# Expert gates from rounded one-hots in a high and a low part, and delta-rule scalings spread over four jobs

## Chip, cores and metric

The program runs on one core of one Trainium2 chip. Its metric is the device time of one execution in microseconds (us), the median of the runs shown. TensorE (PE), VectorE (DVE), ScalarE (ACT) and GpSimd (POOL) run their own instruction streams in order and meet at semaphores; SyncE (SP) issues most DMAs.

## What is computed

One block with attention, a state-space mixer, memory attention and an expert layer is followed by two layers with a state-space duality mixer, latent attention, a gated delta rule and an MLP. There are 512 tokens of width 1024. Two places matter here.

The expert layer scores 128 first keys and 128 second keys for each of 8 heads, takes the best 16 pairs, and weighs 16384 experts by them:

```
sv, si = lax.top_k(s, PEER_TOPK)                      # per side, 16 of 128
top, pos = lax.top_k(cand, PEER_TOPK)                 # 16 of the 256 sums
g = jax.nn.softmax(top, axis=-1)
act = jax.nn.gelu(jnp.einsum('thkd,td->thk', u_tab[e], xb))
return jnp.einsum('thk,thkd->td', (g * act), v_tab[e])
```

The delta rule solves, per head and chunk of 128 tokens, a triangular system, and needs the values and keys of each head turned (tokens on partitions) and scaled by beta and by decays.

## The kernel before

**The expert layer (`choose_and_dot`).** For 384 of the 512 tokens all experts are computed densely. The stage multiplies the tokens with 128 weight tiles ("dots"); a tile is 8 chunks, a chunk three products of 128x128 weights with 384 tokens (high x high, low x high, high x low, all in the rounded format fp32r; lines 104 to 106). For every tile, ACT makes the high part of the weights (line 541) and DVE or POOL the low part (lines 553 and 562), PE multiplies, and ACT applies Gelu (line 1889).

Beside it a gate matrix is built. For each token there is a matrix 128x128 over (second key, first key) that holds the gate of every chosen pair. It is the product of two one-hot matrices over the 128 chosen pairs: `hotB`, which is 1 where the pair's second key is the column, and `hotA`, which is the gate where its first key is the column. Both are fp32. Tokens are taken in groups of four. For a group, DVE makes `hotA` with four instructions (is_equal, then mult; line 2031) and `hotB` with one (line 2033), PE multiplies (`gates`, line 1851, four products in fp32), and ACT copies the bank to the gate block (`fill`, line 1894). Both one-hots have two buffers (`HOTS = 2`), so DVE may be two groups ahead; the banks allow PE four groups ahead of ACT.

There are three blocks of 32 groups (blocks 1, 2, 3; block 0 has none, its tokens go another way). PE's order in a block is written out: some tiles (`EARLY_DOTS`, 13 or 14), three transposes of the chosen keys and gates (line 1861), one more tile, then 32 times a group's gates and five chunks. ACT's order for a group is `fill(g)`, and after each tile `after_dot` (a high part and a Gelu); five tiles end in eight groups. DVE's order for a group is the one-hots, one dot product of gathered rows (line 2018), and a low part when one is due. Between the gate stages DVE chooses the pairs of the next block.

**The delta rule (`delta_rule`).** Each of two layers runs it for two halves of four heads, so it runs four times. A half inverts its triangular matrices in 24 jobs (6 levels by 4 heads). A job is, in order: POOL makes a masked matrix (line 3136), PE a product `w` (line 3018), ACT a copy of it (line 3159), PE a product `v` (line 3031), DVE an update (line 3245), PE a transpose back (line 3051), and DVE two masked copies (lines 3215 and 3250). PE's loop issues `w(j+1)`, then `v(j)`, then `turn_back(j-1)`. In every fourth job (4, 8, 12, 16) PE also turns one head: 4 transposes of values and 4 of keys in one go (line 3043, between `w` and `v`). ACT scales the turned values with four instructions after its copy of one job (line 3166) and the turned keys with four after the copy of the next (line 3173); the second set waits for DVE, which first reads the turned keys for `gdn_kd` (line 3257).

Of the kernel before, what the change touches and what calls it, by code (L numbers as in the profile page):

```python
# [11 lines left out]
ALU = mybir.AluOpType  # L12
# [1697 lines left out]
def choose_and_dot(nc, dram, weights, xnH, xnL, iota, room, qT, keys, hT, scratch, banks, ident, spare, rstd, pairs, A, act_pair):  # L1710
# [7 lines left out]
    with ExitStack() as held:  # L1718
# [3 lines left out]
        hotA, hotB = sb("first_hot", [P, HOTS, TOKENS, PK]), sb("second_hot", [P, HOTS, TOKENS, PK])  # L1722
# [52 lines left out]
        with stage(nc, "spilled scored kept dve_step logits exps gates_ready turned laid hot used tokens_done block_filled "  # L1775
                       "activated block_stored x_turned x_laid rows_ready rows_used pairs_activated " + " ".join(names)) as (
                block, spilled, scored, kept, dve_step, logits, exps, gates_ready, turned, laid, hot, used, tokens_done, filled,
                activated, block_stored, x_turned, x_laid, rows_ready, rows_used, pairs_activated, *act_stored, early_loaded, early_weighed, early_high):
# [40 lines left out]
            def _(pe):  # L1819
# [26 lines left out]
                def gates(m):  # L1846
                    pe.wait_ge(hot, m + 1)
                    if m >= 4:
                        pe.wait_ge(filled, m - 3)
                    for k in range(TOKENS):  # L1850
                        last = nc.tensor.matmul(banks[2 + m % 4][:, k * P:(k + 1) * P], hotB[:, m % HOTS, k, :], hotA[:, m % HOTS, k, :],
                                                start=True, stop=True)
                    last.then_inc(tokens_done, 1)
# [17 lines left out]
            def _(act):  # L1871
# [18 lines left out]

                def fill(t, g):
# [7 lines left out]
                for t in range(TT):  # L1899
# [6 lines left out]
                    for k, dst in enumerate((first, second, gateT)):  # L1906
                        nc.scalar.copy(dst[:, t * P:(t + 1) * P], banks[6][:, k * P:(k + 1) * P]).then_inc(laid, 1)
                    after_dot(first_dot[t] + EARLY_DOTS[t])
# [3 lines left out]
                    for g in groups_of(t):  # L1912
                        fill(t, g)
                        while (done + 1) * DC <= (g + 1 - groups_of(t)[0]) * chunks_beside(t):
# [32 lines left out]
            def _(dve):  # L1947
# [22 lines left out]
                def choose(t):  # L1970
# [13 lines left out]

                    cand = s1[:].rearrange("p (h two) n -> p h (two n)", two=2)
# [35 lines left out]
                for t in range(TT):  # L2021
                    choose(t)
                    dve.wait_ge(laid, 3 * t + 3)
                    lows = [i for i in on_vector if gate_dot[t] < i - 1 < first_dot[t + 1]]
                    for g in groups_of(t):
# [4 lines left out]
                        for k in range(TOKENS):  # L2030
                            v.tensor_scalar(hotA[:, m % HOTS, k, :], iota, first[:, n + k:n + k + 1], gateT[:, n + k:n + k + 1],
# [873 lines left out]
def delta_rule(nc, dram, psum, layer, yT, vT, small, cum, row_parts, pick, smallN, cumN, col, cst, ones, ring, weights, rstd, banks, ident, scratch, tools,  # L2905
# [3 lines left out]
    with ExitStack() as held:  # L2909
# [56 lines left out]
        for hb in range(2):  # L2966
# [7 lines left out]
            with stage(nc, "rows_spread products_done masked exps ends_done dve_step banks_used ends_exp odd_turned packed halves_loaded "  # L2974
                           "pool_step firsts_by_pool first_by_dve kbs_ready level_ready w_done w_copied v_done updated t_turned t_copied "
                           "kv_turned v_scaled k_decayed k_scaled n_turned n_made m_made odd_made solved u_copied wt_copied "
# [3 lines left out]
                    turned, v_scaled, k_decayed, k_scaled, n_turned, n_made, m_made, odd_made, solved, u_copied, wt_copied,  # L2980
# [518 lines left out]
```

## Time and profile before

| what | value |
|---|---|
| median of 3 runs | 4693.05 us (4687.57 to 4697.0) |
| the profiled execution's own time | 4697.76 us |
| its span, first to last instruction | 4695.7 us |
| mean granted TensorE clock | 0.984 of full speed |
| busy share PE / DVE / ACT / POOL | 95% / 67% / 36% / 21% |
| gate stages, 868 to 1335 us | three blocks |
| jobs of the delta rule | four times some 41 us, from 2081.7, 2169.1, 3454.5 and 3542.4 us |

A busy share counts the time in which an engine has an instruction under way. Matmuls overlap in the pipeline, so a busy PE can still be paced by something else; the distances between starts tell more. One fp32 matmul is recorded as two pairs of a weight load (PEld) and a matmul, one rounded matmul as one pair.

### The profile page before, as it was taken

Reading aid. Unit: us, or ns where it says so; the run is one execution under the profiler, and the core shown is the slowest. Engines: PE = TensorE matmul, PEld = TensorE weight load, DVE = VectorE, ACT = ScalarE, POOL = GpSimd, SP = SyncE. Lnnn points to the kernel's source line nnn. Section 1 sums busy time; section 2 is a strip of 40 time slices with the busy share of each in tenths; the row PEclk is TensorE's granted clock in tenths of the full one; section 3 lists DMA queues with packets and bytes.
Section 4 is the critical chain, followed back from the end, with each engine's and each line's share of the span. In section 5 each row is a group of like instructions: output and inputs, shape, how many; then the busy total and the mean of one; then the engine's idle time right before and its main releaser. Section 6 shows DMA issues by size and latency. Waiting matters only on the chain. (4 is left out here: it accounts for less than half of the span.)

```text
span 4695.7 us, 60725 instructions
## 1 busy us (share of the span) xinstructions
PE 4484.2 (95%) x23048; PEld 3821.8 (81%) x23048; DVE 3126.7 (67%) x5382; ACT 1712.0 (36%) x2853; POOL 970.1 (21%) x934
## 2 busy tenths in 40 slices
PE   9889899999999999988999999999988999999999
PEld 7428689999999999877777778888877777878887
DVE  6576757899978888876555665533776655665443
ACT  4414433334333333433333343422423424353332
POOL 4661005664633333022000011000022010020000
PEclk9999999999999999989999999999999999999999
DMA  3002125798989999410222213233201221313332
GB/s 117 27 36 93 52 90 164 254 304 278 308 294 354 335 340 338 141 35 19 86 70 66 77 50 114 93 96 98 90 5 46 86 80 41 94 46 111 100 95 81
DMA packets 236465, 610.74 MB, mean 130 GB/s; under 512 B 23312, under 2 KB 108560, under 8 KB 235024
## 3 DMA queue, kind: packets, MB, share of 16 engines
q1 hardware_dynamic: 199312, 472.62, 31.4%
q0 software_dynamic: 36864, 134.23, 7.9%
q8 instruction: 185, 3.03, 0.3%
q14 instruction: 104, 0.85, 0.1%
HBM read 557.22 MB, written 49.55 MB: 129 GB/s over the span
## 5 line engine op out<-in xcount | busy, mean ns | idle before, releaser
L553 DVE TENSOR_TENSOR weight_low<-ring,weight_high 128x1024 fp32r<-128x1024 f32 (+2 forms) x648 | 759.9, 1173 | 940.3 <-PE banks L106 888.5
L541 ACT CAST weight_high<-ring 128x1024 fp32r<-128x1024 f32 (+2 forms) x728 | 730.0, 1004 | 541.8 <-PE banks L106 530.7
L104 PE MATMUL banks<-x_high,weight_high 128*128 128x512 f32 x1856 | 758.0, 408 | 30.1 <-DVE weight_low L553 17.0
L106 PE MATMUL banks<-x_high,weight_low 128*128 128x512 f32 x1856 | 726.5, 391 | 0.0
L105 PE MATMUL banks<-x_low,weight_high 128*128 128x512 f32 x1856 | 726.4, 391 | 0.0
L104 PEld LDWEIGHTS banks<-x_high,weight_high 128*128 128x128 f32 x1856 | 350.7, 189 | 122.5 <-issue 26.8
L553 POOL TENSOR_TENSOR weight_low<-ring,weight_high 128x1024 fp32r<-128x1024 f32 (+1 forms) x22 | 50.4, 2295 | 1927.6 <-PE banks L106 1844.9
L105 PEld LDWEIGHTS banks<-x_low,weight_high 128*128 128x128 f32 x1856 | 351.0, 189 | 82.1 <-issue 10.6
L106 PEld LDWEIGHTS banks<-x_high,weight_low 128*128 128x128 f32 x1856 | 350.4, 189 | 74.7
L104 PE MATMUL banks<-xn_high,weight_high 128*128 128x384 f32 x1024 | 353.6, 345 | 16.4 <-POOL weight_low L562 15.7
L105 PE MATMUL banks<-xn_low,weight_high 128*128 128x384 f32 x1024 | 343.1, 335 | 0.0
L106 PE MATMUL banks<-xn_high,weight_low 128*128 128x384 f32 x1024 | 343.1, 335 | 0.0
L104 PE MATMUL banks<-act_high,weight_high 128*128 128x384 f32 x688 | 233.1, 339 | 2.3 <-PEq L61 2.3
L106 PE MATMUL banks<-act_high,weight_low 128*128 128x384 f32 x688 | 232.4, 338 | 0.0
L105 PE MATMUL banks<-act_low,weight_high 128*128 128x384 f32 x688 | 232.4, 338 | 0.0
L1700 POOL DMA_INDIRECT rows_v<-in_peer_v,pair_rows x128 | 152.2, 1189 | 369.1 <-DVE pair_sum L2204 327.4
L1700 POOL DMA_INDIRECT scratch<-in_peer_u_rows,pair_rows x128 | 172.1, 1344 | 225.4 <-DVE pair_weight L2018 214.3
L104 PEld LDWEIGHTS banks<-xn_high,weight_high 128*128 128x128 f32 x1024 | 193.1, 189 | 22.4 <-POOL weight_low L562 21.5
L562 POOL TENSOR_TENSOR weight_low<-ring,weight_high 128x256 fp32r<-128x256 f32 x232 | 193.1, 865 | 59.0 <-PE banks L106 58.7
L104 PE MATMUL banks<-up_high,weight_high 128*128 128x512 f32 x512 | 199.2, 389 | 0.0
L105 PE MATMUL banks<-up_low,weight_high 128*128 128x512 f32 x512 | 199.2, 389 | 0.0
L106 PE MATMUL banks<-up_high,weight_low 128*128 128x512 f32 x512 | 199.2, 389 | 0.0
(679 smaller groups left out, 9707.3 us busy)
## 6 DMA issues: line engine op xcount, KB each, us to landing
ring<-in_peer_u SPq DMA_DIRECT2D x128, 512.0 KB, 4.6
ring<-in_peer_v SPq DMA_DIRECT2D x128, 512.0 KB, 5.5
ring<-in_w_up SPq DMA_DIRECT2D x64, 512.0 KB, 3.6
ring<-in_w_down SPq DMA_DIRECT2D x64, 512.0 KB, 3.5
ring<-in_w_gate SPq DMA_DIRECT2D x48, 512.0 KB, 3.6
acts<-dot_act SPq DMA_DIRECT2D x124, 192.0 KB, 4.0
activations<-acts SPq DMA_DIRECT2D x124, 192.0 KB, 5.6
ring<-in_w_gdn_in SPq DMA_DIRECT2D x34, 512.0 KB, 3.6
```

Of the source, the lines that this page charges most:

```text
L104: nc.tensor.matmul(out, w_high, x_high, start=start, stop=False)
L105: nc.tensor.matmul(out, w_high, x_low, start=False, stop=False)
L106: return nc.tensor.matmul(out, w_low, x_high, start=False, stop=stop)
L541: self.nc.scalar.copy(self.wH[:, g % HIGHS, 0:kc * P], self.ring[:, g % SLOTS, 0:kc * P]).then_inc(self.high_made, 1)
L553: ops.tensor_tensor(self.wL[:, g % LOWS, 0:kc * P], self.ring[:, g % SLOTS, 0:kc * P], self.wH[:, g % HIGHS, 0:kc * P].bitcast(F32), ALU.s ...
L562: last = ops.tensor_tensor(self.wL[:, g % LOWS, w], self.ring[:, g % SLOTS, w], self.wH[:, g % HIGHS, w].bitcast(F32), ALU.subtract)
L1700: self.nc.gpsimd.indirect_dma_start(out, None, table, where).then_inc(self.loaded[row_home(k, turn)], 16)
```

## The change

In the expert layer both one-hots get the rounded type, and the gate is split: `hotA` holds the gate's high (rounded) part and is made by ACT, and a new `hotL` holds the rest and is made by DVE with the same instructions as `hotA` before. ACT makes a group's `hotA` with four `Abs(iota - first)` and, after these are complete, four `Relu(gate - gate * distance)`. PE multiplies `hotB` with both and adds in the bank: eight rounded products for the four fp32 ones. Per block there are also three more small ACT instructions and one of DVE. ACT makes the first two groups right after the transposes are copied, ahead of the next tile's `after_dot`, and then group g+2 after `fill(g)`.

In the delta rule the transposes of values come in jobs 4, 8, 12, 16 and those of keys one job later. ACT's scalings come two to a job over four jobs; DVE's `gdn_kd` and `gdn_qg` come one job later.

The diff without the lines that only name semaphores:

```diff
--- before.py
+++ after.py
@@ -1719,7 +1719,10 @@
         def sb(name, shape, dt=F32):
             return held.enter_context(nc.sbuf_tensor(name, shape, dt))
         first, second, gateT = spare[:, 0, :], spare[:, 1, :], rstd
-        hotA, hotB = sb("first_hot", [P, HOTS, TOKENS, PK]), sb("second_hot", [P, HOTS, TOKENS, PK])
+        hotA, hotB = (sb(n, [P, HOTS, TOKENS, PK], F32R) for n in ("first_hot", "second_hot"))
+        hotL = nc.alloc_sbuf_tensor_at("first_hot_low", [P, HOTS, TOKENS, PK], F32R, offset=SCORES_AT)
+        gate_high = sb("gate_high", [P, P], F32R)
+        offsets, negated = first[:, 0:P], second[:, 0:P]
         s1 = nc.alloc_sbuf_tensor_at("pair_scores", [P, 2 * PH, PK], F32, offset=SCORES_AT)
         sv = sb("key_top", [P, 2 * PH, TOP])
         si = sb("key_index", [P, 2 * PH, TOP], U32)
@@ -1773,9 +1776,9 @@
...
@@ -1845,11 +1848,14 @@
 
                 def gates(m):
                     pe.wait_ge(hot, m + 1)
+                    pe.wait_ge(first_ready, m + 1)
                     if m >= 4:
                         pe.wait_ge(filled, m - 3)
                     for k in range(TOKENS):
-                        last = nc.tensor.matmul(banks[2 + m % 4][:, k * P:(k + 1) * P], hotB[:, m % HOTS, k, :], hotA[:, m % HOTS, k, :],
-                                                start=True, stop=True)
+                        nc.tensor.matmul(banks[2 + m % 4][:, k * P:(k + 1) * P], hotB[:, m % HOTS, k, :], hotA[:, m % HOTS, k, :],
+                                         start=True, stop=False)
+                        last = nc.tensor.matmul(banks[2 + m % 4][:, k * P:(k + 1) * P], hotB[:, m % HOTS, k, :], hotL[:, m % HOTS, k, :],
+                                                start=False, stop=True)
                     last.then_inc(tokens_done, 1)
 
                 for t in range(TT):
@@ -1888,6 +1894,17 @@
                         act.wait_ge(act_stored[n % 4], 16 * (n // 4))
                     nc.scalar.activation(A[:, n % 4, :], banks[n % 2][:, 0:DENSE], ACT.Gelu).then_inc(activated, 1)
 
+                def build(t, g):
+                    m, n = place[t, g], g * TOKENS
+                    for k in range(TOKENS):
+                        last = nc.scalar.activation(hotA[:, m % HOTS, k, :], iota, ACT.Abs, bias=offsets[:, n + k:n + k + 1])
+                    last.then_inc(distances, 1)
+                    act.wait_ge(distances, m + 1)
+                    for k in range(TOKENS):
+                        last = nc.scalar.activation(hotA[:, m % HOTS, k, :], hotA[:, m % HOTS, k, :].bitcast(F32), ACT.Relu, scale=negated[:, n + k:n + k + 1],
+                                                    bias=gate_high[:, n + k:n + k + 1].bitcast(F32))
+                    last.then_inc(first_ready, 1)
+
                 def fill(t, g):
                     m = place[t, g]
                     act.wait_ge(tokens_done, m + 1)
@@ -1905,12 +1922,22 @@
                     act.wait_ge(turned, t + 1)
                     for k, dst in enumerate((first, second, gateT)):
                         nc.scalar.copy(dst[:, t * P:(t + 1) * P], banks[6][:, k * P:(k + 1) * P]).then_inc(laid, 1)
+                    if groups_of(t):
+                        nc.scalar.mul(offsets, banks[6][:, 0:P], -1.0).then_inc(laid_aside, 1)
+                        nc.scalar.copy(gate_high[:], banks[6][:, 2 * P:3 * P]).then_inc(laid_aside, 1)
+                        act.wait_ge(laid_aside, 3 * blocks.index(t) + 2)
+                        nc.scalar.mul(negated, gate_high[:].bitcast(F32), -1.0).then_inc(laid_aside, 1)
+                        act.wait_ge(laid_aside, 3 * blocks.index(t) + 3)
+                        for g in groups_of(t)[:HOTS]:
+                            build(t, g)
                     after_dot(first_dot[t] + EARLY_DOTS[t])
                     if t in blocks[1:]:
                         act.wait_ge(block_stored, 16 * PARTS * blocks.index(t))
                     done = 0
                     for g in groups_of(t):
                         fill(t, g)
+                        if g + HOTS in groups_of(t):
+                            build(t, g + HOTS)
                         while (done + 1) * DC <= (g + 1 - groups_of(t)[0]) * chunks_beside(t):
                             after_dot(gate_dot[t] + done)
                             done += 1
@@ -1982,6 +2009,8 @@
                     top16(link, 2 * PH, scores[t], sv, si)
                     link(v.tensor_tensor(marked[:], si[:], marks[:].unsqueeze(1).to_broadcast([P, 2 * PH, TOP]), ALU.bitwise_or))
 
+                    if t in blocks[1:]:
+                        dve.wait_ge(tokens_done, place[t - 1, P // TOKENS - 1] + 1)
                     cand = s1[:].rearrange("p (h two) n -> p h (two n)", two=2)
                     by_side = sv[:].rearrange("p (h two) a -> p h two a", two=2)
                     link(v.tensor_tensor(cand.rearrange("p h (a b) -> p h a b", b=TOP),
@@ -2021,6 +2050,11 @@
                 for t in range(TT):
                     choose(t)
                     dve.wait_ge(laid, 3 * t + 3)
+                    if groups_of(t):
+                        block = slice(t * P, (t + 1) * P)
+                        dve.wait_ge(laid_aside, 3 * blocks.index(t) + 2)
+                        v.tensor_tensor(gateT[:, block], gateT[:, block], gate_high[:].bitcast(F32), ALU.subtract).then_inc(low_laid, 1)
+                        dve.wait_ge(low_laid, blocks.index(t) + 1)
                     lows = [i for i in on_vector if gate_dot[t] < i - 1 < first_dot[t + 1]]
                     for g in groups_of(t):
                         m = place[t, g]
@@ -2028,7 +2062,7 @@
                             dve.wait_ge(tokens_done, m - HOTS + 1)
                         n = t * P + g * TOKENS
                         for k in range(TOKENS):
-                            v.tensor_scalar(hotA[:, m % HOTS, k, :], iota, first[:, n + k:n + k + 1], gateT[:, n + k:n + k + 1],
+                            v.tensor_scalar(hotL[:, m % HOTS, k, :], iota, first[:, n + k:n + k + 1], gateT[:, n + k:n + k + 1],
                                             ALU.is_equal, ALU.mult)
                         v.tensor_tensor(hotB[:, m % HOTS], iota.unsqueeze(1).to_broadcast([P, TOKENS, PK]), bc(second[:, n:n + TOKENS], PK),
                                         ALU.is_equal).then_inc(hot, 1)
@@ -3031,17 +3065,23 @@
                             last = nc.tensor.matmul(banks[4 + j % 2][:, p * P:(p + 1) * P], second_half(x)[:, p, :], Wb[j % 2][:, p, :], start=True, stop=True)
                         last.then_inc(v_done, 1)
 
-                    def turn(x):
+                    def turn_v(x):
                         if x:
-                            pe.wait_ge(v_scaled, x)
-                            pe.wait_ge(k_scaled, x)
+                            pe.wait_ge(v_scaled, 2 * x)
                         else:
                             pe.wait_ge(t_copied, B4)
-                        for n, src in enumerate((vT[:, heads[x]], xp[:, 4 + heads[x] // 2])):
-                            for t in range(TT):
-                                s = slice(t * P, (t + 1) * P)
-                                last = nc.tensor.transpose(banks[6 + n][:, s], src[:, s], ident)
-                        last.then_inc(turned, 1)
+                        for t in range(TT):
+                            s = slice(t * P, (t + 1) * P)
+                            last = nc.tensor.transpose(banks[6][:, s], vT[:, heads[x], s], ident)
+                        last.then_inc(v_turned, 1)
+
+                    def turn_k(x):
+                        if x:
+                            pe.wait_ge(k_scaled, 2 * x)
+                        for t in range(TT):
+                            s = slice(t * P, (t + 1) * P)
+                            last = nc.tensor.transpose(banks[7][:, s], xp[:, 4 + heads[x] // 2, s], ident)
+                        last.then_inc(k_turned, 1)
 
                     def turn_back(j):
                         pe.wait_ge(updated, j + 1)
@@ -3075,8 +3115,11 @@
                             turn_first(B4 - 1)
                         if j + 1 < total:
                             w(j + 1)
-                        if j >= 4 and j % 4 == 0 and j // 4 <= B4:
-                            turn(j // 4 - 1)
+                        x, step = divmod(j - 4, 4)
+                        if 0 <= x < B4 and step == 0:
+                            turn_v(x)
+                        if 0 <= x < B4 and step == 1:
+                            turn_k(x)
                         v(j)
                         if j >= 1:
                             turn_back(j - 1)
@@ -3161,17 +3204,17 @@
                         if 0 <= x < B4:
                             h = heads[x]
                             if step == 0:
-                                act.wait_ge(turned, x + 1)
-                                for t in range(TT):
+                                act.wait_ge(v_turned, x + 1)
+                            if step == 2:
+                                act.wait_ge(k_decayed, x + 1)
+                                act.wait_ge(kbs_ready, 1)
+                            for t in (2 * (step % 2), 2 * (step % 2) + 1):
+                                if step < 2:
                                     last = nc.scalar.activation(vb[:, x, t, :], tiles4(banks[6])[:, t, :], ACT.Copy,
                                                                 scale=smallN[:, t, BETA_ROWS + h:BETA_ROWS + h + 1])
-                                last.then_inc(v_scaled, 1)
-                            if step == 1:
-                                act.wait_ge(k_decayed, x + 1)
-                                act.wait_ge(kbs_ready, 1)
-                                for t in range(TT):
+                                else:
                                     last = nc.scalar.activation(kb[:, x, t, :], tiles4(banks[7])[:, t, :], ACT.Copy, scale=kbs[:, t, x:x + 1])
-                                last.then_inc(k_scaled, 1)
+                            last.then_inc(v_scaled if step < 2 else k_scaled, 1)
 
                     for x in range(B4):
                         act.wait_ge(solved, x + 1)
@@ -3252,10 +3295,10 @@
                             v.tensor_tensor(final(x, 1), inverse(x), half_mask(LEVELS), ALU.mult).then_inc(odd_made, 1)
                         y, step = divmod(j - 5, 4)
                         if 0 <= y < B4:
-                            if step == 0:
-                                dve.wait_ge(turned, y + 1)
+                            if step == 1:
+                                dve.wait_ge(k_turned, y + 1)
                                 v.tensor_tensor(kd[:, y], tiles4(banks[7]), bc(g_end[:, y, :], P), ALU.mult).then_inc(k_decayed, 1)
-                            if step == 2:
+                            if step == 3:
                                 v.scalar_tensor_tensor(qg[:, y, :], xp[:, heads[y] // 2, 0:T], GDN_SCALE, eg[:, y].rearrange("p t n -> p (t n)"),
                                                        ALU.mult, ALU.mult)
                     turned_half(total - 1)
```

## Rows read from the trace of the kernel before

**Rows 1.** The page: busy time of each engine over the span.

```profile
PE 4484.2 (95%) x23048; PEld 3821.8 (81%) x23048; DVE 3126.7 (67%) x5382; ACT 1712.0 (36%) x2853; POOL 970.1 (21%) x934
```

**Rows 2.** Busy time by stretch: start and end, length, busy us and instructions of PE, PEld, DVE, ACT, POOL, clock.

```profile
900.00:950.00 50.00, 50.00 (x332) 50.00 (x331) 50.00 (x109) 19.95 (x31) 19.80 (x14) 1.00 0.85 282
```

**Rows 3.** Timeline, 878 to 911 us: start, length, engine, line, tiles, shape, count.

```profile
881.09 1.11 DVE L2031 TENSOR_SCALAR first_hot<-iota,spare,rstd 128x128 f32<-128x128 f32 x4
...
883.26 1.05 PE L1851 MATMUL banks<-first_hot,second_hot 128*128 128x128 f32 x8
...
884.50 0.34 PE L106 MATMUL banks<-xn_high,weight_low 128*128 128x384 f32 x1
884.68 0.33 PE L104 MATMUL banks<-xn_high,weight_high 128*128 128x384 f32 x1
...
909.00 1.11 DVE L2031 TENSOR_SCALAR first_hot<-iota,spare,rstd 128x128 f32<-128x128 f32 x4
...
911.22 0.49 PE L1851 MATMUL banks<-first_hot,second_hot 128*128 128x128 f32 x3
```

**Rows 4.** Groups of ACT instructions, 868 to 1335 us: busy us, mean ns, idle before.

```profile
L541 ACT CAST weight_high<-ring 128x1024 fp32r<-128x1024 f32 x89 | 93.6, 1052 | 0.0
L1894 ACT COPY gate_block<-banks 128x512 f32<-128x512 f32 x96 | 56.4, 587 | 178.1 <-PE banks L1851 178.1
L1889 ACT ACTIVATE dot_act<-banks 128x384 f32<-128x384 f32 x88 | 43.5, 494 | 99.9 <-PE banks L106 99.5
```

**Rows 5.** ACT instructions by form over the span, with and without an operand per partition.

```profile
L2625 ACT CAST ident_r<-ident 128x128 fp32r<-128x128 f32 x2 | 0.6, 282 | 0.0
L541 ACT CAST weight_high<-ring 128x256 fp32r<-128x256 f32 x32 | 13.0, 407 | 41.8 <-PE banks L106 40.3 <-DMA ring<-in_w_mla_uv 1.4
L609 ACT ACTIVATE mem_high<-qkT,vec 128x256 fp32r<-128x256 f32 x8 | 3.3, 496 | 1.0 <-PEq L61 1.0
```

**Rows 6.** Timeline, 2090 to 2098 us: a delta-rule job with key scalings, and one after.

```profile
2090.68 0.68 DVE L3257 TENSOR_TENSOR gdn_kd<-banks,gdn_end 128x512 f32<-128x512 f32 x1
...
2091.40 1.14 ACT L3173 ACTIVATE hT<-banks,gdn_kbs 128x128 f32<-128x128 f32 x4 [1.80 <-DVE gdn_kd L3257]
...
2092.42 0.66 ACT L3159 COPY ring<-banks 128x256 f32<-128x256 f32 x2
2092.86 0.71 PE L3031 MATMUL banks<-ring,gdn_Tt 128*128 128x128 f32 x4 [1.44 <-ACT ring L3159]
```

**Rows 7.** Timeline of DVE, 1036 to 1048 us: dependent instructions, and the wait before the one-hots.

```profile
1037.09 0.29 DVE L2005 TENSOR_REDUCE gate_sums<-to_turn 128x8 f32<-128x128 f32 x1
1037.41 0.20 DVE L2006 RECIPROCAL gate_sums<-gate_sums 128x8 f32<-128x8 f32 x1
...
1044.08 2.26 DVE L2031 TENSOR_SCALAR first_hot<-iota,spare,rstd 128x128 f32<-128x128 f32 x4 [6.13 <-ACT rstd L1907]
```

**Rows 8.** Weight loads: the timeline at 2012.65 us, and groups by form over the span.

```profile
2012.65 2.54 PEld L155 LDWEIGHTS banks<-columns,gdn_squares 128*128 128x128 f32 x21
...
L1851 PEld LDWEIGHTS banks<-first_hot,second_hot 128*128 128x128 f32 x768 | 98.6, 191 | 3.1 <-DVE second_hot L2033 3.1
...
L106 PEld LDWEIGHTS banks<-xn_high,weight_low 128*128 128x128 f32 x1024 | 192.6, 188 | 0.0
```

**Rows 9.** Table loads of ACT over the span.

```profile
L1889 ACT ACT_TABLE_LOAD x5 | 6.4, 1283 | 0.1
L1904 ACT ACT_TABLE_LOAD x4 | 5.1, 1283 | 0.1
```

**Rows 10.** Delta-rule jobs: busy by stretch, waits of the first stretch, and the copies over the span.

```profile
2081.68:2122.08 40.40, 33.65 (x255) 32.49 (x255) 30.50 (x73) 16.77 (x56) 18.22 (x21) 0.89 0.00 1
...
ACT hT L3173 <- DVE gdn_kd L3257: 8.4, 4, 2.4
...
PE banks L3031 <- ACT ring L3159: 6.7, 4, 1.9
...
  PE banks L3031: 27.0, 16
```

More of the change, by code:

```diff
@@ L1775, in choose_and_dot @@
         with stage(nc, "spilled scored kept dve_step logits exps gates_ready turned laid hot used tokens_done block_filled "
-                       "activated block_stored x_turned x_laid rows_ready rows_used pairs_activated " + " ".join(names)) as (
+                       "activated distances_made first_hot_ready laid_aside low_laid block_stored x_turned x_laid rows_ready rows_used pairs_activated " + " ".join(names)) as (
                 block, spilled, scored, kept, dve_step, logits, exps, gates_ready, turned, laid, hot, used, tokens_done, filled,
-                activated, block_stored, x_turned, x_laid, rows_ready, rows_used, pairs_activated, *act_stored, early_loaded, early_weighed, early_high):
+                activated, distances, first_ready, laid_aside, low_laid, block_stored, x_turned, x_laid, rows_ready, rows_used, pairs_activated, *act_stored, early_loaded, early_weighed, early_high):
             @block.sync
@@ L2975, in delta_rule @@
                            "pool_step firsts_by_pool first_by_dve kbs_ready level_ready w_done w_copied v_done updated t_turned t_copied "
-                           "kv_turned v_scaled k_decayed k_scaled n_turned n_made m_made odd_made solved u_copied wt_copied "
+                           "v_turned k_turned v_scaled k_decayed k_scaled n_turned n_made m_made odd_made solved u_copied wt_copied "
                            "state_ready ws_done v_new_ready o_done ds_done o_copied decayed") as (
@@ L2979, in delta_rule @@
                     pool_step, firsts_by_pool, first_by_dve, kbs_ready, level_ready, w_done, w_copied, v_done, updated, t_turned, t_copied,
-                    turned, v_scaled, k_decayed, k_scaled, n_turned, n_made, m_made, odd_made, solved, u_copied, wt_copied,
+                    v_turned, k_turned, v_scaled, k_decayed, k_scaled, n_turned, n_made, m_made, odd_made, solved, u_copied, wt_copied,
                     state_ready, ws_done, v_new, o_done, ds_done, o_copied, decayed):
```

## The prediction

> **What bounds the kernel now.** I read the busy line of the page first [rows 1]: PE 95%, DVE 67%, ACT 36%. These are means over stages, so they only say that ACT looks free. The change acts in two stages, and each has to be read for itself.
>
> The gate stages come next, by busy time per stretch [rows 2]. In a typical 50 us PE is busy 50.00, DVE 50.00 and ACT 19.95. The reader is to see that two engines are full, not one. The timeline gives their pace [rows 3]. PE starts the products of one group at 883.26 and those of the group eight later at 911.22: 27.96 / 8 = 3.495 us a group. DVE starts its one-hots at 881.09 and eight groups later at 909.00: 27.91 / 8 = 3.489 us, and in this stretch nobody makes it wait. So PE paces the stage and DVE follows 0.006 us behind. ACT needs 19.95 / (50 / 3.495) = 1.39 us a group and then waits for PE: 178.1 us in all before its fills [rows 4].
>
> In the delta rule I read the waits and the timeline of one job [rows 6, 10]. ACT holds its next copy back behind four key scalings, which themselves wait 1.80 us for DVE's gdn_kd, and PE stands 1.44 us before it can start the product that reads the copy. Over the four halves PE waits 27.0 us in 16 such places, one for each head turned.
>
> **Gates, PE's part.** A chunk is three products 0.173 us apart (884.50 to 884.68 is one step; five chunks and the gates must fill 3.495). Fifteen take 2.59 us, which leaves 3.495 - 2.59 = 0.90 us for a group's gates. They are eight pairs of load and matmul now and eight after: four fp32 products of two pairs each against eight rounded ones of one pair. What is streamed gets shorter, but what of the weight load? Where the moving side is one column, 21 loads take 2.54 us in all, so (2.54 - 0.19) / 20 = 0.117 us apart; the gate products are (1.05 - 0.28) / 7 = 0.11 apart with 128 columns [rows 3, 8]. So the load alone explains the distance today, and a load for a rounded product is recorded at 188 ns against 191 [rows 8]. I take the eight pairs at the same 0.90 us. Bounds: 8 x 0.065 = 0.52 if only the streaming counted (0.173 for 384 columns is 0.120 more than for 128 at the same rate per column, less what a product has of fixed cost), and 8 x 0.22 = 1.76 if a short rounded product streamed twice as slowly as an fp32 pair. Even the lower bound brings nothing by itself: DVE's 3.489 us stands right behind PE's 3.495, and DVE keeps its four small instructions and its large one. At most 0.006 x 96 = 0.6 us can be gained here while DVE stays.
>
> **Gates, ACT's part.** This is new and large: eight activations for each group. No row shows one from SBUF with 128 columns and two operands per partition, so I build it up. Without such an operand 128x128 takes 282 ns. One operand per partition costs 496 - 407 = 89 ns more at 256 columns [rows 5]. So an Abs (bias) takes 0.371 us and a Relu (scale and bias) 0.460. Instructions in a row overlap: four scalings of 368 ns took 1.14 us [rows 6], so they start (1.14 - 0.37) / 3 = 0.257 apart, an overlap of 0.111. Then four Abs are 3 x 0.260 + 0.371 = 1.15; the wait until they are complete adds 0.03 (a dependent instruction on DVE starts at 1037.41 after one that ended at 1037.38 [rows 7]); four Relu are 4 x 0.349 = 1.40. Together 2.58 us a group, and with the old 1.39 ACT needs 3.97 us where PE needs 3.495. ACT becomes the bound. Bounds: all eight as cheap as the PSUM scalings, 8 x 0.257 + 0.11 + 0.03 = 2.20, gives 3.59; no overlap at all, 4 x 0.371 + 0.03 + 4 x 0.460 = 3.35, gives 4.74.
>
> It will be more than the bare sum, because ACT's work comes in lumps in a fixed order. Three groups in eight have only fill and build, 0.50 + 2.58 = 3.1 us, and there ACT waits for PE. The other five carry a high part and a Gelu on top, 3.1 + 1.36 = 4.4 us. If nothing of the idle time is carried over, the mean is (5 x 4.4 + 3 x 3.5) / 8 = 4.1. A late high part then stops DVE at its low part, the next one-hots are queued behind that on DVE, which has no slack, and PE waits for them, which makes the next fill late. I put 0.1 us on this and take 4.20 us a group. The two groups of lead are used up within the first few groups. Cost: (4.20 - 3.495) x 96 = +68 us. By the bare sum of 3.97 it is +46, by the low end with lumps some +20, by the high end +120.
>
> The Trainium skill prices the same thing in "ScalarE: Activation LUTs", What ACT_TABLE_LOAD costs: about 93 ns for each pointer operand, and about 93 ns of overlap between activations in a row. The rows agree on the first (89 ns) and show a little more overlap (111 ns). By the page's figures an Abs would come every 0.293 us and a Relu every 0.386, the build would be an estimated 2.9 us, ACT 4.3, and with the same lumps the cost near +90.
>
> The small things: three extra ACT instructions a block (about 0.3 us each) and the first two builds (5.2 us) come before a tile's high part, while PE has one tile of 4.14 us and its first gates ahead of it; the third tile's high part is then made about 2 us later than now, still before PE asks for it. DVE's subtraction (0.29 us) falls after a wait of 6.13 us [rows 7] for ACT and moves by at most 1 us; this happens beside PE's tile. I count 0, at most +1 a block. DVE's new wait before it writes the candidates is for products of the block before, long done: 0.
>
> **Delta rule.** PE's transposes stay eight a head, four in each of two jobs. On ACT, kd's wait stays one job behind, but two scalings instead of four stand between it and the next copy: 1.14 - 2 x 0.257 = 0.63 us follow instead of 1.14, so each of the 16 stalls shrinks by 0.51 us, 8 us in all. Half of the values' transposes no longer stand ahead of the same product v, which lets DVE start 0.2 us earlier: 3 us. So -11, and I take -12 with a little of the clock: the mean granted clock is 0.89 in these stretches [rows 10], so idle time there is followed by half-speed stretches (1.2 GHz instead of 2.4), and shorter stalls may avoid some. Bounds: 0, if the wait for kd simply ends later by as much, since kd too moves by a job; -27 if all waits of rows 10 went.
>
> **The sum.** The profiled execution took 4697.76 us: a span of 4695.7 and 2.06 around it. 4697.8 + 68 - 12 = 4753 us. It lies 4.7 us above the median of the runs shown, so the forecast for the median is 4693.05 + 56 = 4749; I say 4748.
>
> **Rivals.** (1) ACT keeps up, and the kernel is faster. If an activation of 128 columns comes every 0.2 us or less, whatever its operands, the build is under 1.7 us, ACT needs about 3.1 a group, and even the lumps (0.50 + 1.7 + 1.36 = 3.56) are carried by the two groups of lead. The gates then cost 0, the delta rule gives 12: 4681. For it: ACT is idle 60% of the stage. Against it: no row has 128 columns and an operand closer than 0.257 us. It decides at a build of about 2.0 us. (2) A short rounded product streams slowly: 1.76 us for eight pairs makes PE's group 2.59 + 1.76 = 4.35, above ACT's 4.20, and with both near each other about 4.7: +115 - 12, so 4796. For it: no row has a rounded product under 256 columns. Against it: from 512 down to 256 columns nothing of the kind shows. (3) Abs or Relu lie in another table set than Gelu: then 60 groups have two loads of 1.283 us [rows 9], 154 us on top of ACT, the engine that paces: 4748 + 154 = 4902. The stage mixes Gelu, copies and casts without such loads now; only Exp brings them, four times. The same page of the Trainium skill (Table sets: the hidden batching unit) says that relu and abs are filled into every set, by which this rival would be void; no row here shows either function. (4) ACT is the bound, but the lumps even out and the lead absorbs much: at 3.7 to 3.85 a group, +20 to +34, 4701 to 4715.
>
> **Chances.** Forecast with its lumps 0.56 (own range 4728 to 4785); rival 4 0.18; rival 1 0.13; rival 2 0.08; rival 3 0.04; that the change does nothing on either side 0.01. The range 4692 to 4802 leaves out rival 1 for the most part and rival 3. What this kernel's runs can tell from no change is about 0.2%, 9.4 us. Faster by more than that is most of rival 1: 0.13. Within it, what is left of rival 1 and the foot of rival 4: 0.05. Slower: 0.82.
>
> **What would show it.** In the changed profile the starts of a group's products should be 4.0 to 4.4 us apart, unevenly, ACT busy 85% or more between 870 and 1400 us, and DVE idle in the gate stretches, where now it is full, waiting for weight_high. ACT should no longer wait much for PE before its fills. The eight gate pairs should still take about 0.9 us; if they take 0.5, the pace should not follow. In the delta rule the longest job should shrink by half a microsecond. I am wrong if groups stay at 3.5 us apart (an activation is cheaper than any row), if table loads stand between the builds, or if the pairs take over 1 us.

## The result, and the profile after

| | before | after |
|---|---|---|
| median, same chip | 4695.02 us (4687.57 to 4700.41, 4 runs) | 4766.24 us (4761.72 to 4766.32, 4 runs) |
| the profiled execution's span | 4695.7 | 4764.5 |
| its own time | 4697.76 | 4766.25 |

The ratio is 1.0141, 95% interval 1.0122 to 1.0161: slower by 71 us. I had said 4748 with a range of 4692 to 4802. From the median that stood before me, 4693.05, that was 55 us slower.

First the page of the changed kernel, its busy line, and the stretch that [rows 2] show for the kernel before (start and end, length, busy us and instructions of PE, PEld, DVE, ACT, POOL, then clock, DMA share, GB/s):

```profile
PE 4502.1 (94%) x23048; PEld 3819.0 (80%) x23048; DVE 3131.2 (66%) x5385; ACT 1974.0 (41%) x3630; POOL 927.8 (19%) x934
```

```profile
900.00:950.00 50.00, 41.91 (x263) 39.36 (x264) 41.26 (x90) 47.76 (x119) 10.31 (x11) 1.00 0.74 230
```

The page hides it: ACT goes from 36% to 41%, still the least busy but for POOL. The stretch shows it: ACT has gone from 19.95 to 47.76 of 50 us, and PE and DVE, which were full, each stand some 8.5 us.

Then the waits between 868 and 1400 us (who <- whom: us in total, times, longest):

```profile
DVE weight_low L553 <- ACT weight_high L541: 76.6, 52, 3.6
PE banks L1855 <- DVE second_hot L2067: 54.3, 49, 2.9
DVE rstd L2056 <- ACT gate_high L1927: 28.8, 3, 15.7
ACT gate_block L1911 <- PE banks L1857: 18.4, 36, 1.6
```

These are to be read as one chain. ACT, which stood 178.1 us for PE before its fills [rows 4], now stands 18.4. It is late with the high part, DVE stands for that at its low part, and behind the low part on DVE are the next one-hots, for which PE stands.

The order on ACT and DVE in the timeline (start, length, what; the idle time before an instruction in brackets):

```profile
917.00 1.65 ACT L1904 ACTIVATE first_hot<-first_hot,gate_high,spare 128x128 fp32r<-128x128 f32 x4
918.56 1.03 ACT L541 CAST weight_high<-ring 128x1024 fp32r<-128x1024 f32 x1
919.50 0.48 ACT L1895 ACTIVATE dot_act<-banks 128x384 f32<-128x384 f32 x1
919.88 0.57 ACT L1911 COPY gate_block<-banks 128x512 f32<-128x512 f32 x1
920.35 1.28 ACT L1900 ACTIVATE first_hot<-iota,spare 128x128 fp32r<-128x128 f32 x4
921.66 1.65 ACT L1904 ACTIVATE first_hot<-first_hot,gate_high,spare 128x128 fp32r<-128x128 f32 x4
923.68 0.59 ACT L1911 COPY gate_block<-banks 128x512 f32<-128x512 f32 x1 [0.37 <-PE banks L1857]
...
919.63 1.23 DVE L553 TENSOR_TENSOR weight_low<-ring,weight_high 128x1024 fp32r<-128x1024 f32 x1 [1.69 <-ACT weight_high L541]
920.77 1.11 DVE L2065 TENSOR_SCALAR first_hot_low<-iota,spare,rstd 128x128 fp32r<-128x128 f32 x4
921.80 0.68 DVE L2067 TENSOR_TENSOR second_hot<-iota,spare 128x512 fp32r<-128x512 f32 x1
```

A fill takes 920.35 - 919.88 = 0.47 us of ACT, the four Abs 921.66 - 920.35 = 1.31, the four Relu 918.56 - 917.00 = 1.56, a high part with its Gelu 919.88 - 918.56 = 1.32. So a build is 1.31 + 1.56 = 2.87 us. The bare sum of a group is 0.47 + 2.87 + 5/8 x 1.32 = 4.17. From the first to the last group PE's products now take 135.7, 137.4 and 137.5 us in the three blocks, 4.38, 4.43 and 4.44 a step with the slow first ones in it (109.4, 109.1 and 109.0 before).

The groups of ACT over these stages (busy us, mean ns of one, idle before), then PE's products of one group, of which the first four stand here:

```profile
L1904 ACT ACTIVATE first_hot<-first_hot,gate_high,spare 128x128 fp32r<-128x128 f32 x384 | 158.5, 483 | 3.2
L1900 ACT ACTIVATE first_hot<-iota,spare 128x128 fp32r<-128x128 f32 x384 | 123.0, 395 | 0.1
```

```profile
944.15 0.33 PE L1855 MATMUL banks<-first_hot,second_hot 128*128 128x128 f32 x1 [1.19 <-DVE second_hot L2067]
944.32 0.28 PE L1857 MATMUL banks<-first_hot_low,second_hot 128*128 128x128 f32 x1
944.43 0.28 PE L1855 MATMUL banks<-first_hot,second_hot 128*128 128x128 f32 x1
944.54 0.27 PE L1857 MATMUL banks<-first_hot_low,second_hot 128*128 128x128 f32 x1
```

An Abs is recorded at 395 ns and a Relu at 483; the products follow each other 0.11 us apart, as the fp32 ones did [rows 3].

In the delta rule, against [rows 10], the jobs of the first half, and then over the span what DVE waited for PE's product v and PE for ACT's copy:

```profile
2167.47:2203.85 36.38, 32.09 (x255) 30.47 (x255) 29.96 (x72) 16.64 (x56) 17.19 (x21) 0.94 0.00 1
```

```profile
DVE scratch L3288 <- PE banks L3065: 23.1, 34, 1.1
PE banks L3065 <- ACT ring L3202: 17.1, 16, 1.6
```

The four halves take 36.38, 35.50, 36.34 and 35.49 us, 143.7 in all, where they took 40.40, 41.10, 40.79 and 40.54, 162.8.

The account, from the same two executions: the first group starts 1.4 us later, the three blocks take 83.0 us more, the two gaps between them 1.5 more. (The 1.4 can't be told from chance: in a second profiled execution of the same changed kernel, `e9_after_again` below, the first group starts 3.3 us earlier than in this one.) That is +86 at the last gate group. The delta rule gives back 19.1, and what is left over, +2, is spread. 86 - 19 + 2 = 69, the difference of the spans.

### The profile page after: what moved, and what is told of

The parts are those of the page before. It is cut to its first block and busy times, and to the rows that moved or that the text cites. A ratio compares the mean times of both kernels' runs of the same rounds, so it can differ in the third digit from the quotient of the medians.

```text
span 4764.5 us, 61502 instructions
## 1 busy us (share of the span) xinstructions
PE 4502.1 (94%) x23048; PEld 3819.0 (80%) x23048; DVE 3131.2 (66%) x5385; ACT 1974.0 (41%) x3630; POOL 927.8 (19%) x934
## 5 line engine op out<-in xcount | busy, mean ns | idle before, releaser
L104 PE MATMUL banks<-xn_high,weight_high 128*128 128x384 f32 x1024 | 355.6, 347 | 22.2 <-POOL weight_low L562 20.9
L1700 POOL DMA_INDIRECT scratch<-in_peer_u_rows,pair_rows x128 | 133.3, 1042 | 341.1 <-DVE pair_weight L2047 321.3
```

Source lines behind the costliest of these rows:

```text
L104: nc.tensor.matmul(out, w_high, x_high, start=start, stop=False)
L1700: self.nc.gpsimd.indirect_dma_start(out, None, table, where).then_inc(self.loaded[row_home(k, turn)], 16)
```

## The experiments

The ten kernels ran in three sets, each on one chip and beside its own runs of the kernel before: `e1` to `e4` beside 4693.8 us (16 runs), `e5` to `e8` beside 4695.21 (14), `e9` and `e10` beside 4700.67 (7). Ratios are to these. Where two sets are compared, I compare the distances to the kernel before. A pace is the mean from the fourth group of a block on.

**Each part alone.** `e1_delta_only` is the kernel before with the hunks of `delta_rule` alone, `e2_gates_only` with those of `choose_and_dot` alone.

> The delta-rule part alone, gates as before. In the profile of the changed kernel the 24 jobs of the four halves span 36.4, 35.5, 36.3 and 35.5 us where before they span 40.4, 41.1, 40.8 and 40.5: -19 us. If that is the whole of it: 19 us faster than before (0.4%). If the shorter jobs only move a wait to what follows them, less than 10 us.

> The gate part alone, delta rule as before. The starts of the last gate group moved by 86.0 us in the changed kernel, so +86 us against before (1.8%), groups 4.3 to 4.4 us apart. If the two parts helped or hindered each other, the sum with the run of the delta part alone would miss the change's +71.

The delta part alone takes 4676.94 us, ratio 0.9961 (0.9949 to 0.9974): -17. The gates alone take 4775.91, ratio 1.0173 (1.0156 to 1.0190): +82. Both sizes hold. 82 - 17 = 65, against 71 for the whole, and against 60 when the whole ran a second time (`e9_after_again` below): nothing shows that the parts touch each other. With the delta part alone the first half is this:

```profile
2081.00:2116.03 35.03, 30.74 (x255) 29.14 (x255) 29.85 (x72) 16.65 (x56) 17.59 (x21) 0.98 0.00 1
```

The same jobs took 36.38 us in the changed kernel at a granted clock of 0.94. PE stands still for 4.29 us in both; all of the 1.35 us is busy time, 32.09 against 30.74, for the same 255 products.

**The Relu taken away.** ACT makes only the distances, so its build falls from 2.87 to 1.31 us; PE and DVE have the same work. Multiplying the high part by the gate is left out.

```diff
-                    last.then_inc(distances, 1)
-                    act.wait_ge(distances, m + 1)
-                    for k in range(TOKENS):
-                        last = nc.scalar.activation(hotA[:, m % HOTS, k, :], ..., ACT.Relu, scale=negated[...], bias=gate_high[...])
```

> The changed kernel without the second four activations of a group (the multiplication of the high part by the gate is left out). Theory, ScalarE's work paces the gates: its work per group falls by 4 x 0.385 = 1.54 us, from about 4.25 to 2.7, under TensorE's 3.49; groups 3.5 to 3.6 us apart, and the time falls to about 4695 - 19 + 6 = 4682. Rival, the eight rounded products and their sums in the bank are what costs: nothing about them is changed, groups stay at 4.3 us, time near 4766.

It takes 4691.88 us, ratio 0.9986 (0.9973 to 0.9999), groups 3.56 us apart. In the waits ACT is again the one that stands for PE:

```profile
ACT gate_block L1906 <- PE banks L1857: 97.9, 94, 2.7
```

So four instructions of 128 columns on an engine that shows 41% busy, and the wait ahead of them, carry about 75 us: the three blocks take 334.1 us instead of 410.6. The rival falls, since the eight rounded products and their sums in the bank are still there. The 10 us above my number are in part the pace, (3.56 - 3.49) x 96 = 7. In the profiled execution the first group also starts 6.6 us later than that of the delta part alone, in work that the edit does not touch. The first groups of all twelve profiled executions start between 869.4 and 877.6 us, so I take this for chance; its cause is open.

**The high parts first.** The same work, but ACT does a tile's high part and Gelu ahead of the build.

```diff
                         fill(t, g)
-                        if g + HOTS in groups_of(t):
-                            build(t, g + HOTS)
                         while (done + 1) * DC <= (g + 1 - groups_of(t)[0]) * chunks_beside(t):
                             after_dot(gate_dot[t] + done)
                             done += 1
+                        if g + HOTS in groups_of(t):
+                            build(t, g + HOTS)
```

> The changed kernel, but ScalarE makes the weights' high part and the Gelu of a finished tile before it builds the one-hots of group g+2. Theory, part of the loss is the order: VectorE waits 77 us for high parts that stand behind a build, its next one-hots stand behind that, and TensorE waits for them. Then groups should come about 0.12 us closer (4.25 of pure ScalarE work is left) and the time fall by 10 to 17 us, to some 4752. Rival, ScalarE's bare sum alone sets the pace: no change, 4766. Other side: the build comes later, and if TensorE then waits for first_hot, slower by a few us.

> The changed kernel once more, for comparison on one chip with the high parts first. 4762 to 4772; groups 4.33 to 4.39 us apart.

> The changed kernel with the high parts ahead of the build, once more: its profiled execution had shown 19 us less than the changed kernel's, the median of its four 33 us. Theory (only the groups' pace changes, 0.18 to 0.24 us x 96): 4743 to 4749, 17 to 23 us under the changed kernel on the same chip. Rival (a further gain of some 12 us lies outside the gate groups and is there in most executions): 4731 to 4736, and then the profile shows where.

The first time it took 4733.28 us (4 runs), ratio 1.0078 (1.0061 to 1.0095), 33 below the changed kernel, where I had said 10 to 17 and the profiled execution had 19. So both ran again on one chip: 4739.23 (4735.20 to 4742.93) against 4760.71 (4759.27 to 4768.61). That is 21.5 less, and the spans differ by 22.2. The difference fits the pace alone, though both absolute numbers came out below what I had said for them (4743 to 4749, and 4762 to 4772). Above the kernel before, this kernel is +39.5 and +38.6 the two times, the changed kernel +71.2 and +60.0: it is the changed kernel that moved, and what made it move is open. Groups are 4.15 us apart in every block against 4.32 to 4.39. ACT is full, and DVE's longest wait for a high part falls from 3.6 to 1.2 (both views from `e4_high_first`; the second time they show 49.63 us and 1.2):

```profile
900.00:950.00 50.00, 44.36 (x281) 42.33 (x281) 41.97 (x92) 49.60 (x123) 12.21 (x13) 1.00 0.73 237
```

```profile
DVE weight_low L553 <- ACT weight_high L541: 55.6, 57, 1.2
```

4.15 is the bare sum (4.17) within 0.02. The order cost 22 us, the work itself the rest of the gates' loss.

**Who stands behind PE.** Three kernels asked what it is worth that DVE, at 3.489 us a group, stands 0.006 behind PE's 3.495. All three are the kernel before with the delta part. `e5_one_product` has both one-hots rounded and one product a token; the gate's low part is left out.

```diff
-        hotA, hotB = sb("first_hot", [P, HOTS, TOKENS, PK]), sb("second_hot", [P, HOTS, TOKENS, PK])
+        hotA, hotB = (sb(n, [P, HOTS, TOKENS, PK], F32R) for n in ("first_hot", "second_hot"))
```

`e6_second_by_act` moves the other one-hot to ACT, after the high parts: the one without a gate, whose Relu needs no operand per partition and so is one instruction over 512 columns.

```diff
+                    for k in range(TOKENS):
+                        last = nc.scalar.activation(hotB[:, m % HOTS, k, :], iota, ACT.Abs, bias=offsets[:, n + k:n + k + 1])
+                    last.then_inc(distances, 1)
+                    act.wait_ge(distances, m + 1)
+                    nc.scalar.activation(hotB[:, m % HOTS], hotB[:, m % HOTS], ACT.Relu, scale=-1.0, bias=1.0).then_inc(second_ready, 1)
...
-                        v.tensor_tensor(hotB[:, m % HOTS], iota.unsqueeze(1).to_broadcast([P, TOKENS, PK]), bc(second[:, n:n + TOKENS], PK),
-                                        ALU.is_equal).then_inc(hot, 1)
```

`e7_both_light` has both edits (the low part is left out here too).

> The kernel before with the delta-rule part and both one-hots in the rounded format, made by VectorE as before, and a single rounded product for each token (the low part of the gate is left out): four pairs a group on TensorE instead of the eight of the kernel before. Theory (VectorE's 3.49 us a group stood right behind TensorE's 3.49, so taking 0.45 us of a group from TensorE alone brings nothing): groups stay 3.47 to 3.50 us apart and the time is that of the delta part alone, 4677, within 8 us. Rival (TensorE alone bounded the gate groups, and VectorE had room): groups at 3.05 us, 94 groups x 0.44 = 41 us less, 4636.

> The kernel before with the delta-rule part; the second one-hot alone is made by ScalarE, in plain float32, as four distances and one Relu over 512 columns with constant operands, issued after the high parts of the group before; VectorE makes the first one-hot as before, TensorE has its eight passes. ScalarE's group is then 4 x 0.292 + 0.1 + 0.5 + 1.39 = about 3.17 us, VectorE's 2.89, TensorE's 3.49. Theory (TensorE bounds again, and ScalarE is not late at 3.2): groups at 3.49 to 3.52 us, 4677 to 4680. Rival (any building on ScalarE makes the low part late, since the high parts queue behind it): groups at 3.65 or more, 4692 or more, with VectorE waiting for weight_high over 20 us between 868 and 1400 us.

> As the two others together: the second one-hot by ScalarE (four distances, one Relu over 512 columns), the first by VectorE, both in the rounded format, one product a token (the low part of the gate is left out). TensorE about 3.04 us a group, VectorE 2.89, ScalarE 3.17. Theory (the three engines bound the group together, and the longest of the three sets it): groups at 3.17 to 3.25 us, 94 x -0.3 = -23 to -30 us against the delta part alone, 4647 to 4654. Rival (what is gained on the engines is lost to lumps of ScalarE's queue, as in the changed kernel): groups at 3.4 or more, 4668 or more.

They took 4675.38 us (ratio 0.9962, 0.9948 to 0.9977), 4679.52 (0.9967, 0.9958 to 0.9977) and 4645.80 (0.9899, 0.9882 to 0.9915). The delta part alone took 4676.94 on another chip. By the distances to the kernel before, the three are at -19.8, -15.7 and -49.4, the delta part alone at -16.9. Each edit alone brings nothing that can be told, both together 31 to 33 us; the three blocks take 293.9 us instead of 327.5. The same stretch of the three, in this order:

```profile
900.00:950.00 50.00, 46.34 (x275) 43.47 (x274) 50.00 (x109) 21.16 (x33) 20.60 (x15) 1.00 0.90 280
```

```profile
900.00:950.00 50.00, 50.00 (x331) 50.00 (x330) 42.24 (x95) 45.07 (x104) 13.11 (x14) 1.00 0.89 282
```

```profile
900.00:950.00 50.00, 49.74 (x306) 48.74 (x305) 46.90 (x107) 49.49 (x117) 14.57 (x17) 1.00 0.93 309
```

The reader is to see who is full. With one product PE has room and DVE has none: groups 3.48 apart. With the second one-hot on ACT, DVE has room and PE none: 3.51, 3.49 and 3.49. Half of the rival's sign is there, DVE waits 24.2 us for high parts between 868 and 1400 us, but PE waits for DVE's one-hots only 0.2 us. With both, PE and ACT are full together: 3.12, 3.19 and 3.16 in the three blocks, a little under what I had said (3.17 to 3.25, and 4647 to 4654 us). ACT's build in it is this:

```profile
920.90 1.27 ACT L1896 ACTIVATE second_hot<-iota,spare 128x128 fp32r<-128x128 f32 x4
922.20 0.63 ACT L1899 ACTIVATE second_hot<-second_hot 128x512 fp32r<-128x512 f32 x1
922.74 0.57 ACT L1904 COPY gate_block<-banks 128x512 f32<-128x512 f32 x1
```

1.84 us instead of 2.87: the Relu over 512 columns takes 922.74 - 922.20 = 0.54 where four with operands take 1.56. ACT needs 0.47 + 1.84 + 0.83 = 3.14. This is the fastest kernel of the study. Where the gate's low part must stay, it is the delta part alone, 4677.

**What paces a gate product.** The changed kernel with products of 64 columns and the same weight loads (half of each gate matrix is left out).

```diff
+                        out = banks[2 + m % 4][:, k * P:k * P + P // 2]
...
-                        nc.tensor.matmul(banks[2 + m % 4][:, k * P:(k + 1) * P], hotB[:, m % HOTS, k, :], hotA[:, m % HOTS, k, :],
+                        nc.tensor.matmul(out, hotB[:, m % HOTS, k, :], hotA[:, m % HOTS, k, 0:P // 2], start=True, stop=False)
...
```

> The changed kernel with the eight rounded products of a group streaming 64 columns instead of 128 (half of each gate matrix is left out), their weight loads as before. Theory (the pair is bound by its 128-column weight load): the matmuls still follow each other 0.11 us apart in a run. Rival (the streaming of 128 columns sets the 0.11 us): 0.06 to 0.09 us apart. ScalarE bounds the groups either way, so the time stays at 4766 within 10 us.

It took 4768.83 us (one run). Two of its eight products:

```profile
945.00 0.28 PE L1856 MATMUL banks<-first_hot,second_hot 128*128 128x64 f32 x1
945.11 0.28 PE L1857 MATMUL banks<-first_hot_low,second_hot 128*128 128x64 f32 x1
```

Still 0.11 us apart: half the columns bring nothing. That leaves the 128-column load, or a fixed price of any pair. Two places in the traces separate them. The first product of a group comes behind one of 384 columns, and its own load is early. The second product then follows it closely, as here in the kernel without the Relu:

```profile
903.56 0.22 PE L1855 MATMUL banks<-first_hot,second_hot 128*128 128x128 f32 x1
903.62 0.27 PE L1857 MATMUL banks<-first_hot_low,second_hot 128*128 128x128 f32 x1
903.73 0.28 PE L1855 MATMUL banks<-first_hot,second_hot 128*128 128x128 f32 x1
```

That is 0.06 us in 69 of its 96 groups, and 0.03 in 57 of the 96 groups with 64 columns; from then on the loads start 0.11 apart and the products with them. So 128 rounded columns stream in 0.06 us or less. And in the state-space layers of the kernel before, fp32 products have loads of 64 columns, and for a moment two heads overlap on the two halves of the output (their products take turns, 0.05 to 0.06 us apart) before the second goes on alone:

```profile
2784.15 0.27 PE L2738 MATMUL banks<-ssd_L,gdn_v 128*64 128x128 f32 x1
2784.20 0.27 PE L2740 MATMUL banks<-ssd_CE,scratch 128*64 128x128 f32 x1
2784.36 0.38 PE L2740 MATMUL banks<-ssd_CE,scratch 128*64 128x128 f32 x2
```

Pairs with their loads can thus follow each other in half the time, so a pair has no fixed price of 0.11. For the rounded products that leaves the load. For fp32 it does not: the two passes of one head stay (0.38 - 0.27) = 0.11 apart with half the load, and in the kernel before the second pass of a group came no closer than the rest, 0.11 behind the first in 92 of 96 groups. There the streaming of 128 columns alone gives 0.11, and the load gives the same.

## Why the prediction was right, and where its numbers were off

- **Which step decides.** That ACT becomes the bound of a gate group, and that its lateness reaches PE over the high part, DVE's low part and the one-hots, was right. With the Relu gone the pace fell back to 3.56, and with the high parts first, where ACT hardly ever stands, it went to ACT's bare sum.
- **ACT's build: the mis-sized term.** I had 2.58 us, it is 2.87. Two things were small. An Abs took 395 ns and not 371, a Relu 483 and not 460. And they overlap less than the scalings of [rows 6]: four Abs in 1.28 start (1.28 - 0.395) / 3 = 0.295 apart, an overlap of 0.10, four Relu 0.39 apart, an overlap of 0.09; I had taken 0.111. The rest of ACT is 1.30 and not 1.39, so the bare sum is 4.17, where I had 3.97. 0.2 x 96 = 19 us, which is the difference between my +68 and the +86 within a microsecond. The estimate that I set aside, by "ScalarE: Activation LUTs" of the Trainium skill (What ACT_TABLE_LOAD costs), was a build of 2.9 and +90. The trace agrees with the page: 93 ns of overlap against 0.09 to 0.10 measured, and 483 - 395 = 88 ns for one more operand against 93.
- **The lumps.** I put 4.20 - 3.97 = 0.23 us a group on them. The pace with and without them is 4.32 to 4.39 against 4.15, and the two kernels on one chip differ by 21.5 / 96 = 0.22. This term was right.
- **PE's pairs.** Unchanged at 0.11 us apart, as forecast. The reason that I gave, that the load alone explains the distance, holds for the rounded products after; for the fp32 passes before it was only half of it, since their streaming takes 0.11 us as well. That the two are equal is why nothing changed, and that part was luck. That a shorter PE would bring at most 0.6 us while DVE stays was right too: with 4 pairs fewer a group the pace was 3.48 against 3.49, and the time 3 us less by the distances to the kernel before, no change that can be told.
- **The small things.** I had 0 to +1 us a block; each gap between blocks grew by 0.75, and the first group's start scatters by more than that. DVE's wait for the turned keys and gates grew from 26.0 to 28.8 us in three places, 0.9 each, where I had at most 1. No table load was added: lines 1895 and 1921 have 5 and 4, as lines 1889 and 1904 had before [rows 9].
- **The delta rule: the other mis-sized term.** I had -12, it is -19 in the two profiles and -17 as a part alone. PE's stalls went from 27.0 to 17.1 us in 16 places, 0.62 each, where I had 0.51. In all PE stands 17.1 us in the jobs of the four halves where it stood 27.5: 10 us, where I had 8. The other 9 are busy time, 126.6 us instead of 135.4 for the same 1020 products, while the granted clock of the halves rose from 0.88 to 0.90 up to 0.94 to 0.96. I had 3 for DVE starting earlier (its wait for the product v fell from 38.7 to 23.1 us, but a shorter product shortens that wait too) and 1 for the clock. So "a little of the clock" was the term that was too small. (The transposes that no longer stand ahead of v are the four of the keys; I had written "of the values'".) This is an account from two executions and no test; the two halves with 0.94 and 0.98 of the clock above differ in the same way. The wait for kd did move along, as the lower bound feared, and it even grew from 33.8 to 38.9 us in all, but only two scalings follow it.
- **What I had said would show.** Groups unevenly apart (3.6, 4.9 and 4.7 in turn), yes. DVE idle for weight_high, yes. Of ACT I had said 85% or more between 870 and 1400 us; it was 81.5%, since the stretches between blocks count too. Within the first block it is 129.74 of 135.66 us.
- **The rivals.** ACT keeping up fell with a build of 2.87 where 2.0 would have decided. A slow short product is not in the trace, and neither are table loads between the builds. The lumps evening out at 3.7 to 3.85 was not possible, as the bare sum alone is 4.17. The errors partly cancel: +18 for the gates, -7 for the delta rule, +2 left over, together +13 on the profiled time.

## What to carry to other kernels

Before work is moved to an engine that the page shows at a low share, add up its instructions for one turn of the loop in that stage. Here ACT, at 36% of the span, had 1.39 us of work in a 3.5 us turn, and eight more small instructions, 0.3 to 0.4 us apart, took it to 4.17. In an order written by hand the place also counts: put what another engine waits for ahead of what has a buffer of lead. And where two engines pace a stage within 0.006 us of each other, relieve both or neither: either edit alone gave nothing, the two together 31 to 33 us.

## What the runs showed of the hardware that I had not expected

- On ScalarE an activation of 128 columns starts every 0.295 us with one operand per partition and every 0.39 with two; one of 512 columns without any takes 0.54. The same 512 columns in four instructions take 1.18 with one operand and 1.56 with two: for such small tiles the count and the operands weigh more than the columns.
- A rounded product of 64 or 128 columns with a 128-column load comes every 0.11 us, and 0.03 or 0.06 us behind the one before where its load is not what it waits for. An fp32 pass of 128 columns takes 0.11 us also with a load of 64. So splitting one fp32 product into two rounded ones saves nothing, and costs PE at most 0.03 us a group: undisturbed groups come 3.52 us apart in the kernel without the Relu, 3.49 in the kernel before.
- TensorE fell to half its clock in the kernel with 64 columns, after it had stood 1.18 us before a group's products at 944.75 (the changed kernel has such a stop, 1.19 us at 944.15, and kept its clock). In the stretch below the granted clock is 0.57 on the mean, most of it the 1.2 GHz level, and products of 384 columns come 0.32 us apart instead of 0.17. Groups were 4.41 us apart there, 4.32 to 4.39 in the changed kernel. Between 870 and 1400 us its mean granted clock is 0.92, and 0.98 in the changed kernel. Why this kernel lost it more often was not tried.

```profile
946.00:950.00 4.00, 4.00 (x17) 4.00 (x15) 3.50 (x7) 3.97 (x11) 0.94 (x1) 0.57 0.60 177
```
